# A two-model chain on one core: halved squares and moved copies in the lifted norm, GpSimd masks in the column attention

## The reference

```python
x = layer_norm(ALPHA * x + 0.5 * swiglu(x, ffn2_w13[3], ffn2_w2[3]), ln_g[3, 2], ln_b[3, 2])   # end of the first
h = rms_norm_2(x, norm_mix[0])                                                # x * rsqrt(mean(x*x) + eps) * gain
qa, ka, va, u, qm, km, vm, gates = split_in(h @ w_in[0])
# 8 heads with a window of 128 and a sink, 8 heads that see all keys (at 256 tokens there is one block):
s = q @ k.T * 64 ** -0.5 - slope[head] * (t - s_pos);  masked with -inf outside window / causal triangle
p = softmax(s);  o = p @ v
ys = s5_ssm(u, ...)                                                           # the recurrence
x = x + (sigmoid(gates) * [branch outputs]) @ w_out[0];  then a feed-forward and a last norm
```

## Time and profile before

| | us |
|---|---|
| median of 3 runs | 2520.18 (2519.7 to 2521.05) |
| the profiled execution | 2521.28 |
| its span | 2519.5 |
| PE busy | 2466.1 (98%) |
| DVE busy | 1516.8 (60%) |
| ACT busy | 1185.5 (47%) |
| GpSimd busy | 420.3 (17%) |
| mean granted TensorE clock | 0.994 of full |

### The profile page before, as it was taken

One profiled execution on the slowest core, in us unless ns is written; L12 is line 12 of the kernel. 1 busy time (PEld: TensorE's weight loads), 2 busy tenths in 40 slices (PEclk: granted clock), 3 DMA queues, 4 the chain that ended last, 5 costly groups with the idle time before them and its releaser, 6 DMA issues. The chain is left out here.

```text
span 2519.5 us, 32773 instructions
## 1 busy us (share of the span) xinstructions
PE 2466.1 (98%) x13233; PEld 2079.4 (83%) x13233; DVE 1516.8 (60%) x2174; ACT 1185.5 (47%) x1508; POOL 420.3 (17%) x463
## 2 busy tenths in 40 slices
PE   9999999999999999999989999999999999999999
PEld 7888878888888888888877888888878877898998
DVE  5557674464445744644656546546766667897644
ACT  5544554444444544444455445444554445444442
POOL 0002310000001100000231000001249802670000
PEclk9999999999999999999999999999999999999999
DMA  7655445555544455555334555554435542335553
GB/s 246 200 185 155 134 151 184 186 180 185 185 151 140 144 184 186 181 184 186 121 110 152 191 192 169 188 195 155 140 130 190 193 140 95 117 121 198 175 193 126
DMA packets 315575, 418.09 MB, mean 166 GB/s; under 512 B 18858, under 2 KB 273187, under 8 KB 315427
## 3 DMA queue, kind: packets, MB, share of 16 engines
q1 hardware_dynamic: 315426, 416.01, 51.1%
HBM read 414.92 MB, written 1.05 MB: 165 GB/s over the span
## 5 line engine op out<-in xcount | busy, mean ns | idle before, releaser
L474 DVE TENSOR_TENSOR wlo<-raw,whi 128x2048 fp32r<-128x2048 f32 (+1 forms) x397 | 910.2, 2297 | 598.2 <-ACT whi L466 597.4
L466 ACT ACTIVATE whi<-raw 128x2048 fp32r<-128x2048 f32 (+1 forms) x400 | 745.1, 1868 | 454.6 <-DMA raw<-in_ffn_w_dram 392.9
L603 PE MATMUL ps<-whi,xh 128*128 128x512 f32 (+3 forms) x1853 | 695.1, 375 | 8.3 <-DVE wlo L1448 2.2
L605 PE MATMUL ps<-whi,xl 128*128 128x512 f32 (+3 forms) x1853 | 688.0, 371 | 0.0
L604 PE MATMUL ps<-wlo,xh 128*128 128x512 f32 (+3 forms) x1853 | 687.3, 371 | 0.0
L603 PEld LDWEIGHTS ps<-whi,xh 128*128 128x128 f32 x1853 | 350.8, 189 | 74.5 <-issue 9.6
L605 PEld LDWEIGHTS ps<-whi,xl 128*128 128x128 f32 x1853 | 350.5, 189 | 60.0
L604 PEld LDWEIGHTS ps<-wlo,xh 128*128 128x128 f32 x1853 | 350.9, 189 | 57.7
L603 PE MATMUL ps<-whi,oh 128*128 128x512 f32 x944 | 380.0, 403 | 0.0
L605 PE MATMUL ps<-whi,ol 128*128 128x512 f32 x944 | 369.1, 391 | 0.0
L604 PE MATMUL ps<-wlo,oh 128*128 128x512 f32 x944 | 367.9, 390 | 0.0
(11 more groups left out here) (347 smaller groups left out, 2709.5 us busy)
## 6 DMA issues: line engine op xcount, KB each, us to landing
raw<-in_ffn_w_dram SPq DMA_DIRECT2D x350, 512.0 KB, 4.8
raw<-in_ffn_w_dram SPq DMA_DIRECT2D x88, 1024.0 KB, 4.9
raw<-in_w_ff_dram SPq DMA_DIRECT2D x32, 1024.0 KB, 5.2
raw<-in_w_out_dram SPq DMA_DIRECT2D x20, 1024.0 KB, 4.9
raw<-in_w_in_dram SPq DMA_DIRECT2D x20, 1024.0 KB, 5.1
raw<-in_dsa_w_in_dram SPq DMA_DIRECT2D x32, 512.0 KB, 4.6
raw<-in_dsa_w_in_dram SPq DMA_DIRECT2D x12, 1024.0 KB, 5.1
raw<-in_fox_w_in_dram SPq DMA_DIRECT2D x16, 512.0 KB, 4.8
```

The source lines that it names most:

```text
L466: act.activation(hi(u)[:, 0:w], raw[:, (slot[u] + 1) % SLOTS, 0:w], ACT.Copy).then_inc(sem("hi_ready"), 1)
L474: dve.tensor_tensor(lo(u)[:, 0:w], raw[:, (slot[u] + 1) % SLOTS, 0:w], hi(u)[:, 0:w].bitcast(F32), ALU.subtract).then_inc(sem("lo_ready"), 1)
L603: pe.matmul(o, ah, bh, start=start, stop=False, skip_group_check=True)
L605: return pe.matmul(o, al, bh, start=False, stop=stop, skip_group_check=True)
```

## The change

Two places change, and one order with them.

Lifted norm: ACT squares each half as soon as it is made and sums it by itself, scaled by 1/32 ahead of the square, so that the two sums add up to the mean; DVE adds both and eps in one instruction. DVE now scales columns 0 to 511, which PE turns first, and ACT columns 512 to 1023. DVE's statistics of tile 1 (`spread(1)`) move from ahead of the copies of tile 0 to behind them, ahead of the low parts.

Column attention: GpSimd makes the masks with two instructions each, four of them ahead of the first scaling and then two after each pair's scaling; DVE only waits for them. DVE's `turned_p(i)` goes between the two fronts of the next pair. At the end ACT copies `ssm_input`'s results in pair 6 in place of a weight unit, and that unit comes behind `turned_p(7)`; DVE builds Z ahead of its weight unit.

```diff
@@ gpsimd, attention @@
+                    def mask(g):
+                        m = (bias, acc)[g % 2]
+                        if g >= 2:
+                            pool.wait_ge(sem("masked"), b("masked", 0) + g - 1)
+                        slope = -8.0 * float(np.float32(2.0 ** (-8.0 * (g + 1) / 16)))
+                        pool.tensor_scalar(m[:, :], distp[:, :], slope, None, ALU.mult).then_inc(sem("mask_slope"), 1)
+                        pool.wait_ge(sem("mask_slope"), g + 1)
+                        pool.tensor_tensor(m[:, :], m[:, :], (windowp if g < 8 else causal)[:, :], ALU.add).then_inc(sem("mask_made"), 1)
                     turn(0)
+                    for g in range(4 if st["mix"] == "col" else 0):
+                        mask(g)
                     for i in range(NP):
                         scale(2 * i)
                         scale(2 * i + 1)
+                        for g in range(2 * i + 4, min(2 * i + 6, NH) if st["mix"] == "col" else 0):
+                            mask(g)
@@ scalar, lifted norm @@
-                        act.wait_ge(sem("lift_made"), 2 * t + 2)
-                        act.activation(xT[:, :, t * P:(t + 1) * P], xn[:, t, :].rearrange("p (k s) -> p k s", k=KT), ACT.Square,
-                                       accum_out=sm[:, t, 0:1]).then_inc(sem("lift_sum"), 1)
+                        for n in range(2):
+                            act.wait_ge(sem("lift_made"), 2 * t + n + 1)
+                            act.activation(xT[:, 4 * n:4 * n + 4, t * P:(t + 1) * P],
+                                           xn[:, t, 512 * n:512 * n + 512].rearrange("p (k s) -> p k s", k=4), ACT.Square,
+                                           scale=1.0 / 32.0, accum_out=sm[:, t, n:n + 1]).then_inc(sem("lift_sum"), 1)
-                        act.activation(lifted(t, 0), xn[:, t, 0:512], ACT.Identity, scale=rstd[:, t, 1:2]).then_inc(sem("xn_act"), 1)
+                        act.activation(lifted(t, 1), xn[:, t, 512:], ACT.Identity, scale=rstd[:, t, 1:2]).then_inc(sem("xn_act"), 1)
@@ scalar, attention: pair 6, then pair 7 @@
-                            split_hi(act, attn_ahead(st, i))
+                            for m in range(2):
+                                act.wait_ge(sem("unit_used"), st["end"] + m + 1)
+                                act.activation(qk_tm[:, 512 * m:512 * m + 512], ps[:, m, :], ACT.Copy).then_inc(sem("u_moved"), 1)
...
-                            for m in range(2):
-                                act.wait_ge(sem("unit_used"), st["end"] + m + 1)
-                                act.activation(qk_tm[:, 512 * m:512 * m + 512], ps[:, m, :], ACT.Copy).then_inc(sem("u_moved"), 1)
@@ vector, lifted norm @@
-                        dve.tensor_scalar(ve[:, t, 1:2], sm[:, t, 0:1], 1.0 / DM, st["eps"], ALU.mult, ALU.add).then_inc(sem("var_ready"), 1)
+                        dve.scalar_tensor_tensor(out=ve[:, t, 1:2], in0=sm[:, t, 0:1], scalar=st["eps"], in1=sm[:, t, 1:2],
+                                                 op0=ALU.add, op1=ALU.add).then_inc(sem("var_ready"), 1)
-                        dve.tensor_scalar(lifted(t, 1), xn[:, t, 512:], rstd[:, t, 1:2], None, ALU.mult).then_inc(sem("xn_dve"), 1)
+                        dve.tensor_scalar(lifted(t, 0), xn[:, t, 0:512], rstd[:, t, 1:2], None, ALU.mult).then_inc(sem("xn_dve"), 1)
-                    spread(1)
-                    turned(0, lambda: centred(1))
+                    turned(0, lambda: centred(1), None, lambda: spread(1))
@@ vector, attention @@
-                        ch.step(dve.scalar_tensor_tensor(out=m[:, :], in0=distp[:, :], scalar=-8.0 * float(np.float32(slope)),
-                                                         in1=(windowp if g < 8 else causal)[:, :],
-                                                         op0=ALU.mult, op1=ALU.add))
+                        dve.wait_ge(sem("mask_made"), g + 1)
                             front(2 * i + 2)
+                            if col:
+                                turned_p(i)
                             front(2 * i + 3)
-                        turned_p(i)
+                        if not col or i == NP - 1:
+                            turned_p(i)
+                        if col and i == NP - 1:
+                            dve.wait_ge(sem("z_zero"), 1)
+                            build_z(0)
@@ tensor, turn_norm @@
-                for h, name in ((0, "xn_act"), (1, "xn_dve")):
+                for h, name in ((0, "xn_dve"), (1, "xn_act")) if "lift" in st else ((0, "xn_act"), (1, "xn_dve")):
```

More of the change, by code:

```diff
@@ L1410, in rest, with turned @@
                                       xh[:, 4 * h:4 * h + 4, tok].bitcast(F32), ALU.subtract).then_inc(sem("xl_ready"), 1)
-                def turned(t, between=None, ahead_of_last=None):
+                def turned(t, between=None, ahead_of_last=None, ahead_of_rest=None):
                     tok = slice(t * P, (t + 1) * P)
@@ L1434, in turned @@
                             rest(t, 1)
+                    if ahead_of_rest:
+                        ahead_of_rest()
                     for h in range(0 if by_pairs(st, t) else 2):
@@ L1486, in mean_square @@
                     def mean_square(t):
-                        dve.wait_ge(sem("lift_sum"), t + 1)
-                        dve.tensor_scalar(ve[:, t, 1:2], sm[:, t, 0:1], 1.0 / DM, st["eps"], ALU.mult, ALU.add).then_inc(sem("var_ready"), 1)
+                        dve.wait_ge(sem("lift_sum"), 2 * t + 2)
+                        dve.scalar_tensor_tensor(out=ve[:, t, 1:2], in0=sm[:, t, 0:1], scalar=st["eps"], in1=sm[:, t, 1:2],
+                                                 op0=ALU.add, op1=ALU.add).then_inc(sem("var_ready"), 1)
                     def scaled(t):
@@ L1701, in mask_of @@
                             return bias if st["mix"] == "dsa" else causal
-                        if g >= 2:
-                            dve.wait_ge(sem("masked"), b("masked", 0) + g - 1)
-                        slope = 2.0 ** (-8.0 * (g + 1) / 16)
-                        m = (bias, acc)[g % 2]
-                        ch.step(dve.scalar_tensor_tensor(out=m[:, :], in0=distp[:, :], scalar=-8.0 * float(np.float32(slope)),
-                                                         in1=(windowp if g < 8 else causal)[:, :],
-                                                         op0=ALU.mult, op1=ALU.add))
-                        return m
+                        dve.wait_ge(sem("mask_made"), g + 1)
+                        return (bias, acc)[g % 2]
                     def front(g):
@@ L1817, in _ @@
                         if col and i == NP - 1:
-                            dve.wait_ge(sem("z_zero"), 1)
-                            build_z(0)
                             split_lo(dve, st["end"] + 3)
```

## The result

The changed kernel takes 2525.82 us in the median of 15 runs (2520.76 to 2527.41), the one before in the same session 2520.13 us (2516.01 to 2523.01). The ratio is 1.002 with a 95% interval of 1.0013 to 1.0027: 3 to 7 us slower, beyond the predicted range. The profiled execution took 2523.42 us, with a span of 2521.6.

A forecast was written before the change was run, and what follows sets the result against it. PE, busy 98% of the span, was taken to bound the kernel. The terms, +0.8 + 0.5 + 0 - 0.9 + 0.4 = +0.8 us, gave 2522.1 for the profiled execution, 2521.0 us as median; range 2516.4 to 2523.6.

The forecast's parts named there:

- Term 1: Lifted norm: halved squares and earlier copies give -0.55 us, GpSimd masks queueing with DVE cost 1.35; net +0.8 us.
- Term 2: First score reductions to first scaling: masks 2 and 3 stand ahead of GpSimd's scaling; +0.5 us, between 0 and 1.0.
- Term 3: Heads 4 to 9: earlier probability copy gains 0.6 us, masks meeting the weight subtraction lose 0.6; net 0.
- Term 4: Heads 10 to 15: PE's 1.03 us wait goes, head 13's late scaling gives some back; -0.9 us.
- The queueing: Norm: a mask's product delays DVE's scaling up to 0.5 us, its sum the weight half up to 1.0; taken 1.35.
- The -0.6 for the copy: Heads 4 to 9: copying the first head's probabilities between the two reductions shortens PE's 1.57 us wait by 0.6 us.
- the 1.03 us wait: PE's wait at 2137.63 in heads 10 to 15, read as for a probability copy and forecast to go.
- Term 5: Attention's end: two qk_tm copies ahead of the last probability copy, a weight copy behind; BT later by +0.4 us.
- The queueing is short: Rival: weight half gets in ahead of the masks, GpSimd ends them in time; -2.7 us, 2517.5; chance 0.27.
- The clock follows: Rival: PE's longer stop at the norm's second low half brings a lower clock; +2.4 us, 2522.6; chance 0.15.

The follow-up runs named there:

- e8: Kernel before the change, with GpSimd's 128x512 product at line 776 written with one operation in place of two; 2518.97 us in one run.
- e1: Changed kernel with the mask's product on GpSimd written with two operations in place of one; 2521.37 us, ratio 1.0006 to the kernel before.
- e5: Changed kernel with the two-operation mask product and the old ACT and DVE orders at the attention's end; 2520.15 us, ratio 1.0001 to before.
- e3: Kernel before with only the lifted norm's part of the change; 2519.30 us, ratio 0.9995 to before.
- e2: Whole change except the masks, which stay one instruction each on VectorE as before; 2519.80 us, ratio 1.0001 to before.
- e11: Kernel before with the norm's part, and VectorE's masks made as one product from tables holding 1e30 where closed; 2517.87 us, ratio 0.9994.

## Why the prediction was wrong

The step that failed is in term 1, where the mask is priced: "The first lies below the 0.62 us of 512 columns (line 776), I take 0.5". The row is of a product with two operations, and the change writes one with a single operation. No product on GpSimd in before has that form, so its price was unknown and not bounded by this row. It measured 1.17 us (e8: 1.49 for 512 columns), where the two-operation form measured the 0.51 I had taken. Terms 2 to 4 are built on this price, and each came out too low; against the change's +5.7 us, the same kernel with the product at the price that I took (e1, e5) is 0.3 to 1.5 us slower than before by its times. Point by point, from the change's landmarks, with e1 as the kernel that I had in effect priced:

- *Term 1*, forecast +0.8: measured -0.28 (e1 -0.30). The transposes and the first product came as forecast (-0.37, -1.18). The queueing was oversized: it cost 0.25 us (e3 against the change), not 1.35. VectorE's scaling got in first and waited for nothing; only the weight half behind it waited 0.3 us, as these rows of VectorE and GpSimd after show, against the last line of the earlier trace rows:

```profile
2063.09 0.49 DVE L1512 TENSOR_SCALAR qk_tm<-xn,rstd 128x512 f32<-128x512 f32 x1 [0.66 <-POOL rstd L764]
2063.49 1.52 DVE L484 TENSOR_TENSOR wlo<-raw,whi 128x1024 fp32r<-128x1024 f32 x1
```

```profile
2063.14 1.47 POOL L854 TENSOR_SCALAR bias<-masks 128x384 f32<-128x384 f32 x1
2064.69 1.19 POOL L856 TENSOR_TENSOR bias<-bias,masks 128x384 f32<-128x384 f32 x1
```

- *Term 2*, forecast +0.5, bounds 0 to 1.0: measured +1.8 (+1.52 less -0.28), in e1 +0.65. The mechanism was right, including the weight half getting in ahead; the size was that of the product. One part of it failed for another reason: VectorE was to reach the reciprocals 0.6 us earlier, and the first came 43.27 us from the zero where before has 43.31, since the 128x2 sum ahead of it stood behind GpSimd's.
- *Term 3*, forecast 0, bounds -1.6 to +1.0: about +3.0 up to values 4 (+4.53 less +1.52). At the lower clock before and after are even there (a mean of 0.91 from 60 to 80 us in both). e1 has +0.5 (+0.80 at values 4) with 1.00 in that stretch, e5 +2.8 with 0.83, so how much of the +3.0 is the product's form stays open between 0.2 and 2.5 us; against e2, at the change's clock and without masks (+0.23 at values 4), the masks make 4.3 us up to here. The -0.6 for the copy was there (1.0 at values 2), and so was its loss at scores 4, as e2 and e3 show even without masks.
- *Term 4*, forecast -0.9: measured +0.2; e1 gives -1.4 (+0.80 to -0.59). With masks of 2.27 us the scalings of pairs 4 and 6 started right behind a mask. (The row of the 1.03 us wait names "issue", not a copy; the trace bears the reading out, since VectorE's copy ends at 2137.53 and PE starts at 2137.63.)
- *Term 5*, forecast +0.4, bounds 0 to 0.8: measured +0.96, +0.81 in e1. From the last pT to BT it is 6.63 us, as forecast (6.6), but the last pT no longer came 0.45 us earlier:

```profile
2145.29 1.08 ACT L1171 ACTIVATE qk_tm<-ps 128x512 f32<-128x512 f32 x2
2147.05 0.49 ACT L1101 ACTIVATE pT<-ps 128x384 f32<-128x384 f32 x1 [0.67 <-PE ps L2388]
...
2153.68 0.59 ACT L1198 ACTIVATE BT<-ps 128x512 f32<-128x512 f32 x1
```

  pT now waits for PE's transposes, so the copies ahead of it, in the earlier trace rows behind it, are hidden and bring nothing, while the weight half goes behind it. This is the bound that the prediction named (0.8), and not the masks' doing: e2, without them, has the same wait (0.75 us) and the same +0.96.
- *The rivals.* "The queueing is short" was right on the norm and wrong on the whole. "The clock follows" had the sign, not the place: in the norm the first product was early and the longer low stretch there cost nothing by scores 1 (-0.28 us). The low level came where PE already ran late; the last values and the end after, against 0.98 and 0.68 in before's same windows:

```profile
2145.00:2150.00 5.00, 4.06 (x22) 0.50 0.07 25
2150.00:2155.00 5.00, 3.51 (x16) 0.52 0.00 0
```

  It is not what makes the loss: e2, with the same mean clock in each stretch of the norm and the attention, has +1.0 of the +5.5 us.
- *The range.* It took in bounds of queueing but none for the price of an instruction form that no row showed. At the forecast price the sum looks good: e1 stands at +0.22 us at the first state product, against +0.8. That is luck in good part: terms 1 and 4 came out 1.1 and 0.5 us below the forecast and terms 3 and 5 0.5 and 0.4 above it, and e5, which met the clock otherwise, stands at +2.19. The lower end of the range has a slip: the midst of 2515.9 and 2517.5 is 2516.7, not 2516.4, which changes nothing here.

## What to carry to other kernels

Price an instruction only by a row of its own form, operations counted; where there is none, widen the bound by what the engine's other forms spread over, and multiply it by how many stand in one queue ahead of somebody who is waited for. Work is not free on an idle engine if that engine also has a short step on the path: 420 us of 2520 busy said nothing of the 1.9 us for which the first scaling queued. It also lengthens the other engine's shortest steps, which no share of busy time shows. And a wait that is removed ahead of an unchanged chain (here the weight halves) comes back one landmark later.

## What the runs showed of the hardware

- On GpSimd a fp32 product by a number takes 2.3 to 2.4 times as long with one operation as with two (128x384: 1.17 against 0.51 us; 128x512: 1.49 against 0.62). The Trainium skill's page "Perfetto Trace Analysis", section "GPSIMD Engine Instruction", advises trusting start-to-start spacing over the spans of this engine; by that rule, the trace agrees: from product to sum it is 1.25 us (2087.72 to 2088.97) in the change and 0.59 (2084.34 to 2084.93) in e1, each 0.08 over the span.
- A weight half that starts 0.04 us ahead of a GpSimd sum makes it 3.12 us long in place of 1.01, and a 128x2 sum of VectorE behind it then takes 0.98 in place of 0.15. The Trainium skill's page "SBUF — State Buffer", section "Who interferes with whom", says that whoever issues first holds the pair for the whole instruction; the trace agrees, down to instructions of two columns.
- Two profiles that issue alike, with the same wait of 2.78 us, came out of it at different granted clocks (1.00 and 0.66 over the 5 us from 2120 on), and the one was 2.9 us ahead at the next scores.
- A one-input product of 128x384 on VectorE takes 0.35 us alone and 0.78 beside a GpSimd scaling that starts 0.07 us ahead of it (e11).
